# HGRN2 and retention key factors of blocks 1 to 3: transposed by DMA from SBUF to SBUF instead of by TensorE and PSUM

## What is computed

```python
h = rmsnorm(x, g_pre)
rq, rk, rv, rg, hq, hf, hi, hg = split(h @ w_in)        # 8 parts of 512 columns
rq, rk = rotary(rq), rotary(rk) * 128 ** -0.5
f = lb + (1 - lb) * sigmoid(hf)                           # HGRN2: forget gate
hq, hk, hv, logf = silu(hq), 1 - f, hi, log(f)
# by chunk of frames, S is a head's 128 x 128 state, D the decay inside the chunk:
o = ((q @ k.T) * D) @ v + (q * decay_to_here) @ S
S = decay_of_chunk * S + (k * decay_from_here).T @ v
y = x + rmsnorm(concat(silu(rg) * headnorm(o_r), silu(hg) * headnorm(o_h)) @ w_out, g_post)
```

## Time and profile before

| | before |
|---|---|
| median of 3 runs | 389.31 us (389.13 to 390.08) |
| the profiled execution | 392.22 us |
| its span, slowest core (core 2) | 390.7 us |
| its spans, all cores | 385.2 to 390.7 us |
| PE busy | 370.5 us (95%) |
| ACT busy | 294.7 us (75%) |
| DVE busy | 251.0 us (64%) |
| POOL busy | 170.2 us (44%) |

### The profile page before, as it was taken

One profiled execution on the slowest core, in us unless ns is written; L12 is line 12 of the kernel. 1 busy time (PEld: TensorE's weight loads), 2 busy tenths in 40 slices (PEclk: granted clock), 3 DMA queues, 4 the chain that ended last, 5 costly groups with the idle time before them and its releaser, 6 DMA issues.

```text
span 390.7 us, 8583 instructions; the slowest of 8 cores (385.2 to 390.7 us)
## 1 busy us (share of the span) xinstructions
PE 370.5 (95%) x2539; PEld 198.9 (51%) x2539; DVE 251.0 (64%) x401; ACT 294.7 (75%) x852; POOL 170.2 (44%) x249
## 2 busy tenths in 40 slices
PE   6797999999999999899999999999999999999972
PEld 5652444544555555455555556554554445555541
DVE  2455574465987845789774656772866767577563
ACT  3563246787899958988879799968989647799871
POOL 5967621325733615464334233412626633234651
PEclk9897989898999999999999999999999999999998
DMA  7899999997131351000403134095321002014245
GB/s 197 184 160 169 193 179 259 195 195 172 29 107 49 68 163 50 1 0 2 145 21 109 56 111 153 10 224 207 107 84 55 1 2 68 3 55 127 91 126 198
DMA packets 17391, 42.20 MB, mean 108 GB/s; under 512 B 1569, under 2 KB 6817, under 8 KB 17346
## 3 DMA queue, kind: packets, MB, share of 16 engines
q1 hardware_dynamic: 12704, 29.04, 23.7%
q0 software_dynamic: 4496, 12.58, 18.8%
q10 hardware_dynamic: 146, 0.04, 0.1%
HBM read 42.05 MB, written 10.09 MB: 133 GB/s over the span
## 4 chain that ended last, share of the span: by engine, by line
PE 84%; DMA 6%; ACT 4%; issue 2%; POOL 1%; DVE 1%; POOLq 0%; ACTq 0%; SPq 0%; DVEq 0%
PE bank L830 30%; PE bank L760 26%; PE bank L1069 14%; DMA Wc<-w_c 5%; PE bank L1058 2%; PE bank L908 2%; PE bank L938 2%; DMA xs<-xp 2%; PE bank L949 2%; PE bank L928 2%; PE bank L940 2%; PE bank L733 1%; ACT og L876 1%; ACT junk L851 1%; POOL Wq L644 0%
## 5 line engine op out<-in xcount | busy, mean ns | idle before, releaser
L830 PE MATMUL bank<-Wc,xT 128*128 128x512 bf16 (+1 forms) x544 | 130.4, 388 | 2.0 <-DMA Wc<-w_c 2.0
L760 PE MATMUL bank<-xT,Wq 128*128 128x512 bf16 (+3 forms) x656 | 127.1, 349 | 2.2 <-DVE AT L917 0.9
L760 PEld LDWEIGHTS bank<-xT,Wq 128*128 128x128 bf16 x656 | 56.3, 100 | 63.9 <-issue 21.2
L830 PEld LDWEIGHTS bank<-Wc,xT 128*128 128x128 bf16 (+1 forms) x544 | 52.3, 100 | 59.8 <-issue 11.5
L1069 PE MATMUL bank<-Wo,ogT 128*128 128x512 bf16 (+1 forms) x240 | 55.1, 379 | 0.5 <-ACT junk L851 0.5
L876 ACT ACTIVATE og<-otg,rsq 128x128 bf16<-128x128 f32 (+1 forms) x120 | 37.9, 391 | 2.0 <-POOL ms L1081 0.9
L851 ACT ACTIVATE junk<-bank 128x128 bf16<-128x128 f32 (+1 forms) x136 | 35.7, 279 | 2.9 <-PE bank L940 2.0
L775 DVE TENSOR_TENSOR bank<-bank,rotb 128x512 f32<-128x512 f32 (+1 forms) x40 | 23.9, 599 | 21.5 <-ACT tE L773 10.0
L809 POOL TENSOR_TENSOR KT<-tF 128x512 bf16<-128x512 f32 (+1 forms) x20 | 17.6, 881 | 45.7 <-DVE tF L801 42.9
L1069 PEld LDWEIGHTS bank<-Wo,ogT 128*128 128x128 bf16 (+1 forms) x240 | 22.7, 98 | 25.8 <-issue 1.5
L777 POOL TENSOR_TENSOR tB<-tB,rotb 128x512 f32<-128x512 f32 (+1 forms) x20 | 26.9, 1343 | 20.5 <-DVE bank L775 14.0
(11 more groups left out here) (135 smaller groups left out, 608.1 us busy)
## 6 DMA issues: line engine op xcount, KB each, us to landing
xr<-xp SPq DMA_DIRECT2D x18, 512.0 KB, 4.1
yp<-xr SPq DMA_DIRECT2D x16, 512.0 KB, 2.7
xs<-xp SPq DMA_DIRECT2D x10, 512.0 KB, 6.5
Wc<-w_c POOLq DMA_DIRECT2D x8, 512.0 KB, 21.2
Wq<-w_q POOLq DMA_DIRECT2D x7, 512.0 KB, 19.8
rotb<-rot_p SPq DMA_DIRECT2D x4, 512.0 KB, 6.1
Wo<-w_o POOLq DMA_DIRECT2D x4, 512.0 KB, 46.4
xs<-xp POOLq DMA_DIRECT2D x2, 512.0 KB, 28.0
```

Of the source, the lines that this page charges most:

```text
L760: ins = e.matmul(banks[bk][:, c0:c1], lhsT=Wq[:, pc, kc, :], rhs=xT[:, kc, c0:c1], start=(kc == 0), stop=(kc == 7))
L830: ins = e.matmul(banks[bk][0:L, :], lhsT=xT[:, kc, j * L:(j + 1) * L], rhs=Wc[:, seg, kc, :], start=(kc == 0), stop=(kc == 7))
```

## The change

For blocks 1 to 3, `Ktm` is no longer filled by two groups of transposes on TensorE and two evictions on ScalarE. One transposing DMA per chunk, issued on SP, reads the chunk's key factors of all 8 heads from `KT` (128 partitions x 1,024) and writes them transposed into `Ktm` (128 frames x 8 heads x 128). Block 0 keeps its transposes on TensorE, and so does the tile of the running streams.

So that a chunk's source is one contiguous row of 1,024 per partition, `KT` of the prompt blocks is laid out by chunk, head, frame instead of head, frame. `stage_B_ret` and `stage_B_hg` write their 512 frames of a head in four pieces of 128 that lie 1,024 elements apart, in one instruction as before. The DMA waits until the keys of all 8 heads are there and both state products of the chunk before have read `Ktm`. The buffers of the last block that lie in block 2's keys get keys of their own, whose readers are all readers of those keys. The planner counts a transposing DMA as 100 ns on SP and as 1 MB of traffic.

```diff
+                    if name == "dma_start_transpose":
+                        self.cost += 100.0
+                        self.lat += 2300.0
+                        self.nbytes += 4 * 262144
...
+        KTf = [t[:].rearrange("p a l -> p (a l)") for t in KTs]
+        KTv = [t.rearrange("p (c h l) -> p c h l", c=4, h=8) for t in KTf[0:2]]
+
+        def kt_tok(bp, h, nch, T):
+            if bp < 2:
+                return KTv[bp][:, 0:nch, h, :]
+            return KTs[2][:, h, :].rearrange("p (c l) -> p c l", c=nch)[:, :, 0:T]
+
+        def kt_tile(bp, h, j):
+            return KTv[bp][:, j, h, :] if bp < 2 else KTs[2][:, h, :]
...
-            return [("KT", 0, 4 + g)] if state["alt"] else [("Sb", g)]
+            return [("altsb", g)] if state["alt"] else [("Sb", g)]
...
-            return [("KT", 0, 2 * n), ("KT", 0, 2 * n + 1)] if state["alt"] else [("zt", n)]
+            return [("altz", n)] if state["alt"] else [("zt", n)]
...
-            S.op(POOL, lambda e: e.tensor_tensor(out=tok(KT[:, hh, 0:nt]), in0=seg(tF)[:, :, 1:T + 1], in1=seg(tF)[:, :, 0:T],
+            S.op(POOL, lambda e: e.tensor_tensor(out=kt_tok(bp, hh, nch, T), in0=seg(tF)[:, :, 1:T + 1], in1=seg(tF)[:, :, 0:T],
...
-                        ins = e.matmul(banks[BSC][0:L, hq_ * L:(hq_ + 1) * L], lhsT=KT[:, h, cs], rhs=QT[:, h, cs], start=True, stop=True)
+                        ins = e.matmul(banks[BSC][0:L, hq_ * L:(hq_ + 1) * L], lhsT=kt_tile(bp, h, j), rhs=QT[:, h, cs], start=True, stop=True)
...
+                if state["kd"]:
+                    if g == 0:
+                        S.op(SP, lambda e: e.dma_start_transpose(Ktm[0][:].rearrange("p (h d) -> p h d", h=8) if len(Ktm[0].shape) == 2 else Ktm[0],
+                                                                 KTf[bp][:, j * 1024:(j + 1) * 1024]),
+                             reads=[("KT", bp, h) for h in range(8)], writes=kKtm(0) + kKtm(1), dma_key=("Ktd", state["alt"]))
+                else:
+                    bt = S.vbank()
...
+                    state["kd"] = b > 0
                     stage_D(j, d["L"], vs, has_state=not (b == 0 and j == 0))
...
+            if (b, j) == (NBP - 1, 0):
+                for key in (("altz", 0), ("altz", 1), ("altsb", 0), ("altsb", 1)):
+                    S.readers[key] = [r for h in range(8) for r in S.readers[("KT", 0, h)]]
```

More of the change, by code:

```diff
@@ L95, in f @@
                     psum = in_psum(out) or any(in_psum(a) for a in ins)
-                    if name == "dma_start":
+                    if name == "dma_start_transpose":
+                        self.cost += 100.0
+                        self.lat += 2300.0
+                        self.nbytes += 4 * 262144
+                    elif name == "dma_start":
                         try:
@@ L577, in build_nc @@
         real = [st.enter_context(nc.psum_tensor("bank%d" % i, [128, 512], F32)) for i in range(8)]
+        KTf = [t[:].rearrange("p a l -> p (a l)") for t in KTs]
[6 more added lines that the diff above has]
+            return KTv[bp][:, j, h, :] if bp < 2 else KTs[2][:, h, :]
         S = Sched()
-        state = dict(tset=0, stores=[], bp=0, alt=False, last=False, np=0)
+        state = dict(tset=0, stores=[], bp=0, alt=False, last=False, np=0, kd=False)
         AT_ = {False: AT[0], True: QTs[0][:, 0:2, :].rearrange("p a (h t) -> p (a h) t", h=4)}
@@ L769, in stage_B_ret @@
             bp = state["bp"]
-            dst = QTs[bp] if which == 0 else KTs[bp]
             dkey = ("QT", bp, h) if which == 0 else ("KT", bp, h)
@@ L778, in stage_B_ret @@
                  reads=[("tB", ts, 0), ("tB", ts, 64), ("rot", rslot)], writes=[("tB", ts, 0), ("tB", ts, 64)])
-            S.op(DVE, lambda e: e.tensor_tensor(out=dst[:, h, 0:nt], in0=banks[bk][:, 0:nt], in1=tB[ts][:, 0:nt], op=ALU.add),
+            if which == 0:
+                add = lambda e: e.tensor_tensor(out=QTs[bp][:, h, 0:nt], in0=banks[bk][:, 0:nt], in1=tB[ts][:, 0:nt], op=ALU.add)
+            else:
+                cut = lambda t: t.rearrange("p (c l) -> p c l", c=nch)
+                add = lambda e: e.tensor_tensor(out=kt_tok(bp, h, nch, L), in0=cut(banks[bk][:, 0:nt]), in1=cut(tB[ts][:, 0:nt]), op=ALU.add)
+            S.op(DVE, add,
                  reads=[("bank", bk), ("tB", ts, 0), ("tB", ts, 64)], writes=[dkey])
@@ L920, in stage_D, with ktr @@
                      reads=[("bank", BSC), "maskT"], writes=kAT(g))
-                bt = S.vbank()
-                kT = ("bank", bt)
-                def ktr(e, hs=hs, bt=bt):
-                    ins = None
-                    for h in hs:
-                        ins = e.transpose(out=tbf(bt)[0:L, h * 128:(h + 1) * 128], in_=KT[:, h, cs], identity=ident[:])
-                    return ins
-                S.op(PE, ktr, reads=[("KT", bp, h) for h in hs] + ["ident"], writes=[kT])
-                S.op(ACT, lambda e, g=g, bt=bt: e.activation(out=Ktm[0][0:L, g * 512:(g + 1) * 512], in_=tbf(bt)[0:L, g * 512:(g + 1) * 512], func=AF.Copy),
-                     reads=[kT], writes=kKtm(g))
+                if state["kd"]:
[3 more added lines that the diff above has]
+                             reads=[("KT", bp, h) for h in range(8)], writes=kKtm(0) + kKtm(1), dma_key=("Ktd", state["alt"]))
+                else:
+                    bt = S.vbank()
+                    kT = ("bank", bt)
+                    def ktr(e, hs=hs, bt=bt):
+                        ins = None
+                        for h in hs:
+                            ins = e.transpose(out=tbf(bt)[0:L, h * 128:(h + 1) * 128], in_=kt_tile(bp, h, j), identity=ident[:])
+                        return ins
+                    S.op(PE, ktr, reads=[("KT", bp, h) for h in hs] + ["ident"], writes=[kT])
+                    S.op(ACT, lambda e, g=g, bt=bt: e.activation(out=Ktm[0][0:L, g * 512:(g + 1) * 512], in_=tbf(bt)[0:L, g * 512:(g + 1) * 512], func=AF.Copy),
+                         reads=[kT], writes=kKtm(g))
                 def omm(e, g=g, hs=hs, BO=BO):
```

## The result

The changed kernel takes **380.96 us** (median; 380.57 us at best), the kernel before 389.37 us on the same chip: ratio 0.9778, 95% interval 0.9758 to 0.9797, so 8.4 us or 2.2% less. The prediction was 383.5 us with a range of 380.5 to 388.5. The sign held, and the range, by 0.5 us at its lower end. The mechanism held for TensorE's own work, 5.4 of the 8.4 us; the other 3.0 are waits that the forecast had only at an end of its range. The gain was 2.6 us larger than forecast, at the size of the rival "more is gained" (379 to 381).

What follows compares the result with a forecast made beforehand. The prediction took TensorE, busy for 95% of the span, as the bound. Its terms -5.2 - 0.4 - 0.5 + 0.3 = -5.8 us took 389.3 to 383.5 us, with a range of 380.5 to 388.5.

Steps and rivals of the forecast that it cites:

- more is gained: Rival: with less ScalarE work and fewer PSUM bank turns, most of TensorE's 4.2 idle us go; 379 to 381, chance 0.08.
- Removed transposes: Blocks 1 to 3 on TensorE: 24 groups of four transposes go, one in the idle tail; 23 x 0.225 = -5.2 us.
- Evictions that held TensorE: ScalarE's removed evictions, blocks 1 to 3: one place where they held TensorE up, -0.4 us; ends -4.2 and +4.2.
- Work moved into the tail's idle time: End on TensorE: a third group of output products fills the wait for the last norm, -0.5 us; -1.4 to +0.3.
- Transfers: 12 transposing DMAs on SP's queue, taken at 4 us each, bounds 2.0 and 9.5: +0.3 us, ends 0 and +6.0.
- Covers: Time from a transfer's possible start to its chunk's first state product, counted in matmuls: shortest 5.4 us, at block 3's start.
- SP's waits and the layout: Delays on SP's queue are taken up before data is missed, and the new key layout costs nothing: 0 each.
- Late transfers: Rival: state products wait for late DMAs; 399 us at 12 us each, gain gone from about 9.6 us; chance 0.11.
- Gain given back to ScalarE: Rival: ScalarE, VectorE and GpSimd set the pace from 110 to 200 us; 386.5 to 389, chance 0.11.
- The signs: Trace if right: L928, L931 at a quarter, TensorE busy about 5 us less, idle near 4, transfers landing within 5.4 us.

Runs made afterwards that it cites:

- e5_late4: Changed kernel, order kept, with SP issuing four tiny DMAs one after the other and waiting for each ahead of every transposing DMA: 391.05 us.
- e5_layout_only: Changed kernel with the new key layout kept but the transposing DMAs taken out, all transposes and evictions as before, planned anew: 389.49 us.
- e2_act_back: Changed kernel, order kept, with 24 copies of 128x512 in PSUM put back on ScalarE ahead of the head norm's squares: 387.96 us.
- e6_act_gate: Changed kernel, order kept, with 24 copies of 128x512 in PSUM put back on ScalarE ahead of the gate's Silu: 385.54 us.
- e5_late2: Changed kernel, order kept, with SP issuing two tiny DMAs one after the other and waiting for each ahead of every transposing DMA: 384.93 us.

## Why the prediction was right, and where its size was off

- **Removed transposes: -5.2 predicted, -5.36 measured.** Right in size and reason: 5.34 with the old order, 5.25 when put back.
- **Evictions that held TensorE: -0.4 (ends -4.2 and +4.2) predicted; no wait names a removed one, and the middle's idle time fell by 2.13.** This is the term that was wrong in its source and in its size. I priced the one wait whose row named the eviction, but that row is block 0's: the eviction at 121 us in the earlier trace rows is the seventh of block 0's eight, which the change leaves alone. The line below shows the wait behind it on core 5, where the first transposes of block 1's keys come only at 142 us; in the changed kernel such a wait is still there, 0.9 us ahead of L1083. By its own reading the term should have been 0, and that its sign came out is luck. In the old order the evictions' removal gave 0.5 us in the middle, taken back in the tail. But the planner then ordered all engines anew, and with that went the waits of before that had other names, for `xT`, `tC` and `AT`. I had written that all of the idle time could go, and used that only as an end of the range.

```profile
120.18 3.61 PE L760 MATMUL bank<-xT,Wq 128*128 128x512 bf16 x16 [0.40 <-ACT Ktm L931]
```

- **Work moved into the tail's idle time: -0.5 (ends -1.4 and +0.3) predicted, -0.87 measured.** The 1.73 us that were read in the order as moved are 1.71 in the windows; idle fell by half of it. The place was right, the value too small by 0.4.
- **Transfers: +0.3 (at 4 us each, bounds 2.0 and 9.5) predicted; 3.2 us measured, no wait.** The upper bound was five times too dear in its packets: the SP queue gained 12,672 packets, 1,056 per transfer and close to the 1,024 that I assumed, but they took (0.294 x 379.1 - 0.237 x 390.7) x 16 / 12,672 = 0.024 us each, not the 0.117 of the mean packet, which is longer. The fixed 2.0 and 66 x 0.024 = 1.6 make 3.6, near the 3.2. The packets' own records agree: each transfer is 1,024 packets of 256 bytes, 0.023 us each on core 2, and 32 of 4 bytes.
- **Covers.** Counted in the order against measured from issue to first state product: 9.8, 14.8, 15.0, 11.8 against 9.3, 14.3, 13.6, 10.7 in block 1; 12.6 and 7.8 against 11.9 and 7.3 in block 2; 5.4 and 7.6 against 7.0 and 8.0 at the start of block 3. The counted ones are off by 0.4 to 1.6 us, on both sides, since a transfer's turn on SP's queue is not the moment from which I counted; with the measured ones the waits of e5_late4 come out to 0.1 us.
- **SP's waits and the layout: 0 predicted, 0 measured** in the changed kernel (e5_layout_only; no wait names a transposing DMA). SP's hold of 1.25 us per transfer, which was not in the sum, costs nothing here.
- **The rivals.** Late transfers: the mechanism exists, with the waits that the covers give, and it did not occur at 3.2 us. The kernel with four delays is that rival: at 8 to 10 us from a transfer's turn to its landing the gain is gone, where I had put the point at 9.6. Gain given back to ScalarE: did not occur, though e2_act_back and e6_act_gate show how close ScalarE is (+4.6 to +7.0 for 14 us). More gained: this is the time that came, at 0.08 the least likely of the four, but not for the reason that I gave it alone. Without ScalarE's evictions the old order kept nearly all of its idle time; it took the new order too. The order was there to be counted before the run; what its waits would be was not.
- **The signs.** Transposes and evictions are a quarter of before, busy time fell by 5.4 us, and no state product waits for a DMA, as written. Two signs failed: idle time did not stay near 4 us, it fell from 4.8 to 1.8 in middle and tail; and one transfer, (3,3)'s on core 2, took 6.6 us and not under 5.4, behind a cover of 25.

What stays open: whether an order with this little waiting exists for the kernel with all its evictions. In the changed order they cost 4.6 to 7.0 us, and with all work in place the planner found only the order of before.

## What to carry to other kernels

Where the matmul engine is busy without gaps, work taken from it counts in full, and a transposing DMA can carry it if the time between the source's last write and the first reader, counted in matmuls, is longer than its landing (3.2 us for 256 KB here, 6.6 at most). A planner that orders everything anew makes a second term of its own: the same instructions in two orders stood 3.0 and 3.4 us apart here (in the second case mostly one wait for a transfer, behind a changed price in the planner), so that term belongs in the range with its full size, and the frozen order is the run that separates it from the change. Look for the engine that is a close second before calling its relief worthless: it was worth 0.1 to 0.5 us in the old order, and putting it back cost 4.6 to 7.0 in the new one.

## What the runs showed of the hardware

A transposing DMA from SBUF to SBUF of 256 KB held its queue for 1.25 us and moved as 1,056 packets of about 24 ns, landing in 3.0 to 6.6 us (core 2 of the changed kernel).

TensorE's clock fell after a wait of 4.7 us. In e5_late4, the eight 512-column products behind the wait for (3,1)'s transfer (core 1; then windows of length, busy times, clock, DMA share, GB/s):

```profile
336.88 0.59 PE L983 MATMUL bank<-V,QT 128*128 128x128 bf16 x4 [4.71 <-DMA QT<-KT]
337.26 3.37 PE L851 MATMUL bank<-Wc,xT 128*128 128x512 bf16 x8
```

```profile
337.00:339.00 2.00, 2.00 (x9) 0.90 (x8) 1.28 (x3) 0.50 (x1) 0.00 (x0) 0.50 0.50 199
339.00:341.00 2.00, 2.00 (x8) 0.82 (x7) 1.19 (x2) 0.40 (x2) 0.00 (x0) 0.69 0.00 0
341.00:343.00 2.00, 2.00 (x11) 0.87 (x9) 0.00 (x0) 0.87 (x3) 0.00 (x0) 1.00 0.00 0
```

The clock was 0.50 of full speed, 1.2 GHz, and back at 2.4 GHz by 341 us; the eight products took 3.37 us where eight take 1.89 at full clock. That is most of the 2.1 us of busy time by which this run exceeds its waits. All eight cores of this run show it: the wait was 4.3 to 5.2 us, the eight products took 3.1 to 3.6. In e5_late2, where the wait at the same place was 0.9 to 2.5 us, they took 1.89 on all eight cores.
